# Expert blocks of a hierarchical MoE step: all gate products first, all up products behind them in a second PSUM bank

## The reference

```
out = jnp.zeros((n * t_len, d), jnp.float32)
for e in range(N_EXPERTS):                      # 32 experts
    hid = jax.nn.silu(t @ w_gate[e]) * (t @ w_up[e])      # 1024 -> 256
    out = out + combine[:, e:e + 1] * (hid @ w_down[e])   # 256 -> 1024
```

## Time and profile before

| | |
|---|---|
| median of 3 runs | 535.07 us (533.61 to 535.42) |
| the profiled execution, its own time | 534.76 us |
| its span, first to last instruction | 532.9 us |
| TensorE matmul busy | 480.9 us (90%) |
| expert blocks | from 272.2 to about 505 us |
| DMA traffic in all | 141.24 MB |
| mean granted TensorE clock | 0.972 |

### The profile page before, as it was taken

One profiled execution on the slowest core, in us unless ns is written; L12 is line 12 of the kernel. 1 busy time (PEld: TensorE's weight loads), 2 busy tenths in 40 slices (PEclk: granted clock), 3 DMA queues, 4 the chain that ended last, 5 costly groups with the idle time before them and its releaser, 6 DMA issues.

```text
span 532.9 us, 8838 instructions
## 1 busy us (share of the span) xinstructions
PE 480.9 (90%) x3269; PEld 282.0 (53%) x3270; DVE 237.9 (45%) x513; ACT 100.4 (19%) x204; POOL 201.0 (38%) x283
## 2 busy tenths in 40 slices
PE   6999999999999999999689998999898882998883
PEld 3777777777777545545344444443444341444431
DVE  3309999999986422245722212222112210211246
ACT  3331011102104423323311111111111100011114
POOL 3002938938598600111143444333343422244100
PEclk9999999999999999999599999999999996999998
DMA  8995008000000598023969899999999999999577
GB/s 333 310 391 149 0 1 313 3 2 0 1 1 0 189 401 338 39 68 125 412 232 413 296 417 418 412 395 419 420 419 418 419 419 419 421 418 418 219 273 261
DMA packets 34564, 141.24 MB, mean 265 GB/s; under 512 B 10160, under 2 KB 10176, under 8 KB 22249
## 3 DMA queue, kind: packets, MB, share of 16 engines
q1 hardware_dynamic: 28250, 127.91, 61.0%
q0 software_dynamic: 4960, 9.45, 4.8%
q10 hardware_dynamic: 1327, 3.49, 1.8%
HBM read 134.47 MB, written 13.17 MB: 277 GB/s over the span
## 4 chain that ended last, share of the span: by engine, by line
PE 67%; DMA 14%; issue 6%; SPq 4%; DVE 4%; ACT 3%; POOL 1%; DVEq 0%; POOLq 0%; ACTq 0%
PE bank L1289 25%; PE bank L1375 10%; PE bank L1493 7%; PE bank L1513 7%; PE bank L1488 6%; DMA z<-in_w_up 6%; DMA region_x<-in_w_up 6%; PE bank L1296 5%; SPq L412 2%; DMA slot<-y_rows 2%; PE bank L1253 1%; PE bank L1503 1%; PE bank L1441 1%; DVE ua L1183 1%; DVE ua L1185 1%
## 5 line engine op out<-in xcount | busy, mean ns | idle before, releaser
L1289 PE MATMUL bank<-region_h,region_w 128*128 128x256 f32 (+1 forms) x544 | 132.7, 406 | 0.0
L1289 PEld LDWEIGHTS bank<-region_h,region_w 128*128 128x128 f32 x544 | 103.2, 190 | 28.2
L1183 DVE TENSOR_TENSOR ua<-ua,bank 128x128 f32<-128x128 f32 x30 | 8.6, 288 | 171.8 <-ACT ua L648 171.8
L1375 PE MATMUL bank<-region_w,z 128*128 128x512 f32 x128 | 56.7, 596 | 0.2 <-ACT z L593 0.2
L1513 PE MATMUL bank<-region_w,ua 128*32 128x512 f32 x328 | 49.9, 598 | 3.2 <-DVE ua L1185 3.1
L732 POOL TENSOR_TENSOR ub<-region_x 128x512 f32<-128x512 f32 x4 | 31.4, 7840 | 54.9 <-ACT region_x L536 54.9
L942 DVE SCALAR_TENSOR_TENSOR z<-ub,par,z 128x512 f32<-128x512 f32 x60 | 47.6, 794 | 0.0
L805 POOL COPY gcol<-gidx 128x1 uint32 (+1 forms) x30 | 5.4, 179 | 106.5 <-DVE sb_rows L1172 104.0
L942 DVE SCALAR_TENSOR_TENSOR region_x<-ub,par,region_x 128x512 f32<-128x512 f32 x56 | 45.5, 813 | 0.0
L1493 PE MATMUL bank<-region_w,z 128*32 128x256 f32 x512 | 44.3, 400 | 0.0
L1375 PEld LDWEIGHTS bank<-region_w,z 128*128 128x128 f32 x128 | 23.8, 190 | 28.0 <-issue 26.3
(11 more groups left out here) (250 smaller groups left out, 684.0 us busy)
## 6 DMA issues: line engine op xcount, KB each, us to landing
region_w<-in_w_down SPq DMA_DIRECT2D x21, 1024.0 KB, 13.8
region_w<-in_w_gate SPq DMA_DIRECT2D x16, 1024.0 KB, 13.3
region_w<-in_w_up SPq DMA_DIRECT2D x16, 1024.0 KB, 15.3
region_w<-in_w_in SPq DMA_DIRECT2D x3, 2048.0 KB, 21.5
slot<-in_w_gate SPq DMA_DIRECT2D x6, 1024.0 KB, 14.4
slot<-in_w_up SPq DMA_DIRECT2D x6, 1024.0 KB
slot<-in_w_down SPq DMA_DIRECT2D x6, 1024.0 KB, 13.8
region_x<-in_w_up SPq DMA_DIRECT2D x5, 1024.0 KB
```

Source lines behind the costliest of these rows:

```text
L1183: nc.vector.tensor_tensor(hid, sg_m, ps[1][:, P:2 * P], ALU.mult).then_inc(s_hid, 1)
L1289: ins = mm(ps[2 * bank + j][:, 0:LEN[j]], sec[name][:, k, c * P:(c + 1) * P], hT[:, k, CUT[j]], start=(k == 0), stop=(k == KC - 1))
L1375: ins = mm(ps[2 * (t % 2) + j][0:n, :], z[:, k, t * P:t * P + n], w_out_sb[:, k, j * 512:(j + 1) * 512], start=(k == order[0]), stop=(k == ...
```

## The change

The gate products go to bank 1 and signal a semaphore of their own (`s_gate`); behind them the up products go to bank 2 and signal `s_gu`. The 256 moving columns become twice 128. Silu waits for `s_gate`, VectorE's product for both, a gate part is reloaded behind `s_gate` and an up part behind `s_gu`. TensorE waits for an expert's gate part ahead of the gate products, and for its up part only between the two. The one-column product writes bank 0 instead of bank 5. Nothing else differs.

```diff
@@ reload (SyncE)
                     if part == 0:
+                        sp.wait_ge(s_gate, last)
+                    if part == 1:
                         sp.wait_ge(s_gu, last)
@@ block_of (ScalarE)
-                act.wait_ge(s_gu, q * 2 + (b + 1))
+                act.wait_ge(s_gate, q * 2 + (b + 1))
@@ block_of (VectorE)
                 dve.wait_ge(s_silu, q * 2 + (b + 1))
-                nc.vector.tensor_tensor(hid, sg_m, ps[1][:, P:2 * P], ALU.mult).then_inc(s_hid, 1)
+                dve.wait_ge(s_gu, q * 2 + (b + 1))
+                nc.vector.tensor_tensor(hid, sg_m, ps[2][:, 0:P], ALU.mult).then_inc(s_hid, 1)
@@ block_of (TensorE)
-                for k in range(KC):
-                    for h in range(2):
-                        if halves[0] == halves[1]:
-                            ins = mm(ps[1][h * T:(h + 1) * T, 0:2 * P].rearrange("p (w f) -> p w f", w=2), xT[:, k, :],
-                                     wgu[halves[0]][:, :, k, h, :], start=(k == 0), stop=(k == KC - 1))
-                            continue
...
-                ins.then_inc(s_gu, 1)
+                for w, (bank, done) in enumerate(((ps[1], s_gate), (ps[2], s_gu))):
+                    if w:
+                        for i in sorted(set(halves)):
+                            pe.wait_ge(s_wexp[i][1], turn * 16 + 16)
+                    for k in range(KC):
+                        for h in range(2):
+                            if halves[0] == halves[1]:
+                                ins = mm(bank[h * T:(h + 1) * T, 0:P], xT[:, k, :],
+                                         wgu[halves[0]][:, w, k, h, :], start=(k == 0), stop=(k == KC - 1))
+                                continue
...
+                    ins.then_inc(done, 1)
@@ pair (TensorE), for slot i and again for slot i + 1
-                for part in range(2):
-                    pe.wait_ge(s_wexp[i][part], it * 16 + 16)
+                pe.wait_ge(s_wexp[i][0], it * 16 + 16)
```

More of the change, by code:

```diff
@@ L261, in build_step @@
         s_xt = sem("s_xt")
-        s_gu = sem("s_gu")
+        s_gate, s_gu = sem("s_gate"), sem("s_gu")
         s_silu = sem("s_silu")
@@ L1484, in block_of @@
                 pe.wait_ge(s_xt, g + 1)
-                for k in range(KC):
-                    for h in range(2):
-                        if halves[0] == halves[1]:
-                            ins = mm(ps[1][h * T:(h + 1) * T, 0:2 * P].rearrange("p (w f) -> p w f", w=2), xT[:, k, :],
-                                     wgu[halves[0]][:, :, k, h, :], start=(k == 0), stop=(k == KC - 1))
-                            continue
[L1491 to L1495, removed]
-                ins.then_inc(s_gu, 1)
+                for w, (bank, done) in enumerate(((ps[1], s_gate), (ps[2], s_gu))):
[8 more added lines that the diff above has]
+                                continue
+                            for half, i in enumerate(halves):
+                                r0 = h * T + half * H
+                                ins = mm(bank[r0:r0 + H, 0:P], xT[:, k, half * H:(half + 1) * H],
+                                         wgu[i][:, w, k, h, :], start=(k == 0), stop=(k == KC - 1))
+                    ins.then_inc(done, 1)
                 pe.wait_ge(s_mv, g + 1)
-                mm(ps[5][0:32, 0:1], onesb[:, 0:32], onesb[:, 0:1], start=True, stop=True)
+                mm(ps[0][0:32, 0:1], onesb[:, 0:32], onesb[:, 0:1], start=True, stop=True)
                 tokens(0, KC // 4)
@@ L1528, in pair @@
                         block_of(g, (i, i), it)
-                for part in range(2):
-                    pe.wait_ge(s_wexp[i + 1][part], it * 16 + 16)
+                pe.wait_ge(s_wexp[i + 1][0], it * 16 + 16)
                 block_of(after - 1, (i, i + 1), it)
```

## The result

The changed kernel takes **596.29 us** (median of 4 runs, 590.63 to 597.63) against 535.25 us for the kernel before (4 runs, 533.61 to 535.82): ratio 1.112, 95% interval 1.106 to 1.119. It is 61 us slower where 531.9 was forecast, far outside the range. The profiled execution took 595.58 us, its span 593.8.

The account below looks back on a forecast made before the run. Expert weight loads on DMA were taken to bound the block stage; -1.4 us for the stream and -1.8 behind it took the profiled 534.76 to 531.6, as a median 531.9 us, range 529.8 to 538.

Parts of the forecast that it names:

- the loop no longer stays in the instruction buffer: Rival, TensorE's loop: grown body is fetched again at each jump back; +9.0 us at 6.8 us each, 544 us; chance 0.11.
- the prediction's own formula: Shift of the blocks' end if each of three jumps back refetches at price S: 1.3 + 3 S - 12.7 us.
- the reserve: TensorE's three late waits for up weights, 1.5, 9.6 and 1.6 us, 12.7 together, which can absorb slower blocks.
- The sum: Whole kernel: -1.4 us for the earlier stream and -1.8 behind it, -3.2 us in all.
- nothing is fetched again: Loop turns of the kernel before: pauses of 0.93 and 1.07 us, so a jump costs 0.14 and needs no refetch.
- the stream: Expert weight transfers behind 301 us, which set the block stage's pace; claimed to come 1.4 us earlier.
- Products: Gate and up products in 128-column groups: excess fixed per group, whole blocks 4.19 us (+0.39), mixed 4.03 us (+0.32).
- it shrinks with the columns: Rival, gate and up products: the excess per group shrinks with the columns, each block 0.31 us shorter; 530.6 us; chance 0.10.
- TensorE becomes bound by its loads: Rival, gate and up groups: weight loads no longer hidden behind 128 columns; 533.0 us if mild, 543 to 563 otherwise; chance 0.16.
- Silu: Each block: silu runs on bank 1 during the up products, so VectorE's product starts 0.31 us earlier.
- Gate load earlier: Slot 2's gate load after block 3: gate products end 1.52 us earlier, transfers behind 301 us come 1.4 us earlier.
- The moved up wait: Last wait for an up part, near 482.60 us: gate products run before it; -2.10 us, capped at -1.8 by the last down load.

Follow-up runs that it names:

- Experiments 2: TensorE's loop written out in both kernels, so no jumps back: changed kernel 569.45 us (ratio 1.064), kernel before 538.82 us (1.007).
- experiment 4: Kernel before with gate products first only in chosen blocks, one bank, silu behind up; six variants: 534.28 to 545.63 us, ratios 0.999 to 1.019.

## Why the prediction was wrong

- **The step that failed is the chance and price of the rival "the loop no longer stays in the instruction buffer".** It named the cause, the place and the sign that would show it (pauses of microseconds at the turns, over 28 fetches), and had the body at some 2,000 instructions. But it put the limit "just at that edge", gave it 0.11, and priced a refetch at 6.8 us, what one gather needs. The runs showed the body of 1,725 already beyond the limit, and pauses of 10 to 12 us in the changed kernel and 15 to 20 with dead code: two to five fetches in each pause, not one transfer's latency. By the prediction's own formula the measured pauses at the turns give 1.3 + 32.8 - 12.7 = 21.4 us; the other 40 come from the next two points and the mixed blocks, and the reserve was no longer there for them.
- **A step was missing: code that runs once must be fetched too.** The sum held nothing for the growth outside the loop, and the rival spoke of jumps only. Experiments 2 and 4 show 9 us from the written-out blocks alone, and 34 with everything written out. In the changed kernel these pauses outside the turns are 26.8 of the 59.6 us. The pause of 0.93 us at the entry of the loop wasn't a warning of it: no fetch falls into it or into the one of 1.07, so the reading "nothing is fetched again" was right for the kernel before.
- **What a pause costs beyond itself was missing too.** The clock drops to its lower level (0.50 at 397 us, 12 us in all), and slots come free late, so the stream, meant to be 1.4 us earlier, stands still.
- **Products.** The excess per group was not fixed: 118 ns at 128 columns, 12 over the 106. The rival that it shrinks with the columns was right for whole blocks; the rival that TensorE becomes bound by its loads was wrong for them. The Trainium skill ("TensorE: Matmul & The Clock Gate", section on the back-to-back issue gap) has 81 ns for a load and a matmul at 128 columns, 28 over the bare columns; the prediction's estimate from it was 134 ns, and the trace has 118. The mixed blocks were mis-sized the other way: 4.4 to 4.6 us instead of the 4.03 forecast, for a cause left open.
- **Silu.** Right in place: VectorE's product starts 0.11 us behind the up products. Of the 0.31 the block keeps 0.23, since the one-column product and the transposes now wait in the chain.
- **Gate load earlier.** The mechanism is real (1.4 to 1.8 us in experiment 4, 1.5 forecast), but in the changed kernel it never showed: 295.18 - 269.81 = 25.4 us from the stage's first product to the load, 25.3 before. A pause of 1.34 us in block 0 and the slow mixed block took it. Up's load went out 1.9 us behind it (2.0 forecast).
- **The moved up wait** found no wait to shorten. (Its cap was a little too high as well: 498.65 + 2.5 is 501.15, not 501.0, so 1.65 us and not 1.8.) That the run could have been 3.2 us faster falls with it: with four blocks split, 0.8 us were left in the trace and nothing that the timing can tell.

## What to carry to other kernels

Before splitting a product in a loop, count the instructions of the loop's body on that engine, with both passes of an fp32 product and their weight loads: there is a cliff, not a slope, and here it cost 53 us for a hundred instructions. The profile warns of it in two rows, the number of instruction fetches and the "issue" pauses at the turns; if the body fits now, the question for every edit is how much room is left. When the code outside the loop grows, ask which pauses fall ahead of a release that matters.

## What the runs showed of the hardware

- TensorE's loop body is kept up to some 1,625 instructions (22 fetches, none behind the second and third jump back) and is fetched again at each turn from 1,725 on (49); between them, and with the loop at another place in the code, wasn't tried.
- A refetch of such a body costs 15 to 20 us with full DMA queues and 10 to 13 with queues a third busy when it holds dead code, and 10 to 12 or 5.5 to 8 us in the changed kernel. The changed kernel pays less because two or three fetches fall into its pause and four or five into the other; why the dead part asks for more isn't settled. It adds a jump forward out of the code that was fetched, but that is only argued.
- Code executed for the first time isn't free: with two short products in place of one, TensorE stops for 1 to 4.5 us at times; in block 5 it is 3.54 us, and 1.18 under light loads. The Trainium skill ("Runtime: NRT & Kernel Launch", section on instruction fetch mechanics) holds, where it speaks of a buffer of two 16 KiB lines, that fetches are hidden behind the engine's own pace, and that kernels do well to unroll; here TensorE's are not hidden, and unrolling the kernel before cost 0.7%.
- fp32 products of 128 columns in tiles of 64 lose 12 ns per group of two over the 106 of the columns, those of 256 lose 25 over 212. In tiles of 32 a group of four loses 20 ns at 256 columns and 32 to 38 at 128 in the changed kernel (4.41 and 4.6 us for 32 groups), gaps included; without the gaps a split mixed block takes no longer than an unsplit one (7.00 us).
